# Retention's inverse root in two mixers: a power of minus one half on GpSimd instead of a root on ScalarE and a reciprocal on VectorE

## What is computed

```
def multiscale_retention(q, k, v, gate):            # 8 heads of 64, 512 tokens, chunks of 128
    ...
    o = (intra + cross).reshape(B, S, H, D)
    mu = jnp.mean(o, axis=-1, keepdims=True)
    var = jnp.mean(jnp.square(o - mu), axis=-1, keepdims=True)
    o = ((o - mu) * lax.rsqrt(var + GN_EPS)).reshape(B, S, H * D)
    return jax.nn.silu(gate) * o

def hybrid_mixer(x, ...):
    h = x @ w_in                                    # 22 tiles of 128 columns
    ...                                             # sliding-window attention, 8 heads; retention, 8 heads
    return jnp.concatenate([y_attn, y_ret], axis=-1) @ w_out
```

## Time and profile before

| | us |
|---|---|
| median of three runs | 3137.31 |
| lowest, highest | 3136.26, 3140.68 |
| the profiled execution's own time | 3135.46 |
| its span, from first to last instruction | 3134.2 |
| TensorE busy in the span | 3053.6 (97%) |
| VectorE busy | 1415.7 (45%) |
| ScalarE busy | 1173.1 (37%) |
| GpSimd busy | 373.3 (12%) |
| mean granted TensorE clock | 0.992 |

### The profile page before, as it was taken

How to read it: one execution, slowest core, us unless ns; L and a number is a source line. 1 busy time by engine, 2 the same in 40 slices (tenths; PEclk the granted TensorE clock), 3 DMA queues, 4 the chain that set the end, 5 groups by cost and what they waited for, 6 DMA issues and landing times.

```text
span 3134.2 us, 39362 instructions
## 1 busy us (share of the span) xinstructions
PE 3053.6 (97%) x16470; PEld 2554.1 (81%) x16470; DVE 1415.7 (45%) x2118; ACT 1173.1 (37%) x1910; POOL 373.3 (12%) x275
## 2 busy tenths in 40 slices
PE   8999999999999999999999999999999989999999
PEld 7888876788888888886688888899998767788888
DVE  3333465653334433356573333644423667554432
ACT  3322366442224322156553221522223456543321
POOL 0000133300001000024320000200002322110000
PEclk9999999999999999999999999999999999999999
DMA  4223321222232322331113223222233211122232
GB/s 159 95 93 92 100 88 48 75 95 94 93 93 65 121 94 91 94 112 63 61 56 120 94 89 93 68 95 95 85 88 100 81 34 34 35 94 95 94 92 76
DMA packets 76496, 269.62 MB, mean 86 GB/s; under 512 B 8720, under 2 KB 9008, under 8 KB 76064
## 3 DMA queue, kind: packets, MB, share of 16 engines
q1 hardware_dynamic: 74448, 260.08, 25.5%
q0 software_dynamic: 1872, 7.04, 0.7%
HBM read 264.97 MB, written 2.11 MB: 85 GB/s over the span
## 4 chain that ended last, share of the span: by engine, by line
PE 90%; DVE 5%; ACT 3%; issue 1%; DMA 0%; POOL 0%; SPq 0%; DVEq 0%; ACTq 0%
PE psum L376 25%; PE psum L379 25%; PE psum L382 25%; PE psum L437 3%; PE psum L449 2%; PE psum L395 1%; PE psum L399 1%; PE psum L397 1%; PE psum L673 1%; PE psum L2608 1%; DVE x_lo L740 1%; ACT prob L1766 0%; PE psum L1627 0%; PE psum L1649 0%; DVE x L825 0%
## 5 line engine op out<-in xcount | busy, mean ns | idle before, releaser
L332 DVE TENSOR_TENSOR w_lo<-w_raw,w_hi 128x1024 fp32r<-128x1024 f32 (+1 forms) x442 | 551.9, 1251 | 1246.3 <-ACT w_hi L321 1246.1
L376 PE MATMUL psum<-x_hi,w_hi 128*128 128x512 f32 (+1 forms) x2792 | 963.6, 369 | 1.9 <-ACT neg_mean L2679 1.2
L379 PE MATMUL psum<-x_hi,w_lo 128*128 128x512 f32 (+1 forms) x2792 | 947.7, 364 | 0.0
L382 PE MATMUL psum<-x_lo,w_hi 128*128 128x512 f32 (+1 forms) x2792 | 942.9, 362 | 0.0
L321 ACT CAST w_hi<-w_raw 128x1024 fp32r<-128x1024 f32 (+1 forms) x490 | 503.9, 1029 | 1160.2 <-PE psum L382 1125.4
L376 PEld LDWEIGHTS psum<-x_hi,w_hi 128*128 128x128 f32 x2792 | 499.7, 189 | 109.0 <-issue 18.3
L379 PEld LDWEIGHTS psum<-x_hi,w_lo 128*128 128x128 f32 x2792 | 498.8, 189 | 87.7 <-issue 5.5
L382 PEld LDWEIGHTS psum<-x_lo,w_hi 128*128 128x128 f32 x2792 | 499.7, 189 | 84.2
L376 PE MATMUL psum<-h_hi_ffn,w_hi 128*128 128x512 f32 (+1 forms) x792 | 296.9, 375 | 0.0
L379 PE MATMUL psum<-h_hi_ffn,w_lo 128*128 128x512 f32 (+1 forms) x792 | 292.2, 369 | 0.0
L382 PE MATMUL psum<-h_lo_ffn,w_hi 128*128 128x512 f32 (+1 forms) x792 | 290.7, 367 | 0.0
(11 more groups left out here) (384 smaller groups left out, 3428.9 us busy)
## 6 DMA issues: line engine op xcount, KB each, us to landing
w_raw<-in_ffn_gu SPq DMA_DIRECT2D x176, 512.0 KB, 3.2
w_raw<-in_ffn_down SPq DMA_DIRECT2D x64, 512.0 KB, 3.5
w_raw<-in_w_in SPq DMA_DIRECT2D x44, 512.0 KB, 3.2
w_raw<-in_b_gate SPq DMA_DIRECT2D x44, 512.0 KB, 3.2
w_raw<-in_b_up SPq DMA_DIRECT2D x44, 512.0 KB, 3.2
w_raw<-in_b_down SPq DMA_DIRECT2D x32, 512.0 KB, 3.5
w_raw<-in_ffn_down SPq DMA_DIRECT2D x32, 384.0 KB, 3.1
w_raw<-in_b_in SPq DMA_DIRECT2D x24, 512.0 KB, 3.2
```

Of the source, the lines that this page charges most:

```text
L332: nc.vector.tensor_tensor(w_lo[s][:, 0:n], w_raw[r][:, 0:n], w_hi[s][:, 0:n].bitcast(F32), ALU.subtract).then_inc(*w_low_dve.inc(u))
L376: nc.tensor.matmul(out, w_h, hi[:, c], start=first and i == 0, stop=False)
L379: nc.tensor.matmul(out, w_l, hi[:, c], start=False, stop=False)
L382: done = nc.tensor.matmul(out, w_h, lo[:, c], start=False, stop=final and i == n - 1)
```

## The change

ScalarE's step keeps its place and its input but writes the variance (Identity with the same scale and bias) where it wrote the root. VectorE's reciprocal is gone. GpSimd gets a new instruction in its place in the list, which raises the 128x512 tile to the power that stands in a constant column (-0.5, spread over the 512 columns). The constant is one more memset at the start, and GpSimd waits there for it before its next DMA. The second block and the layer norms keep their roots and reciprocals. Line numbers of the changed kernel differ by a few.

```diff
@@ timetable
-                              (e + 2.4, "r_stat", j), (e + 2.5, "o_root", j),
+                              (e + 2.4, "r_stat", j), (e + 2.5, "o_variance", j),
                               (e + 2.7, "o_inverse", j), (e + 3.2, "o_norm", j),
...
@@ mixer_act
-                    elif step == "o_root":
+                    elif step == "o_variance":
                         act.wait_ge(*o_stat.at(item))
                         nc.scalar.activation(o_sq[:], psum[:, banks["r_stat", item][0], :],
-                                             ACT.Sqrt, bias=eps[:, 1:2],
-                                             scale=1.0 / HD).then_inc(*o_root.inc(item))
+                                             ACT.Identity, bias=eps[:, 1:2],
+                                             scale=1.0 / HD).then_inc(*o_variance.inc(item))
...
@@ mixer_dve
-                    elif step == "o_inverse":
-                        dve.wait_ge(*o_root.at(item))
-                        nc.vector.reciprocal(o_sq[:], o_sq[:]).then_inc(*o_inverse.inc(item))
...
@@ mixer_pool
+                    elif step == "o_inverse":
+                        pool.wait_ge(*o_variance.at(item))
+                        nc.gpsimd.tensor_tensor(
+                            o_sq[:], o_sq[:], eps[:, 5:6].to_broadcast([P, SEQ]),
+                            ALU.pow).then_inc(*o_inverse.inc(item))
...
@@ start
+            nc.vector.memset(eps[:, 5:6], -0.5).then_inc(*eps_set.inc(8))
...
+        pool.wait_ge(*eps_set.at(8))
```

More of the change, by code:

```diff
@@ L1536, in mixer_1 @@
             o_stat = signal("o_stat", keys("r_stat"))
-            o_root = signal("o_root", keys("o_root"))
+            o_variance = signal("o_variance", keys("o_variance"))
             o_inverse = signal("o_inverse", keys("o_inverse"))
@@ L1550, in mixer_1 @@
                 "r_kv": lambda j: stated.at((j, NB - 2)), "r_out": o_made.at,
-                "r_sum": o_centred.at, "r_stat": o_root.at, "mean": leave.negated.at}
+                "r_sum": o_centred.at, "r_stat": o_variance.at, "mean": leave.negated.at}
             def pe_wait_side(step, item):
@@ L3055, in build @@
         ones_set = signal("ones_set", [0])
-        eps_set = signal("eps_set", range(8))
+        eps_set = signal("eps_set", range(9))
         start_high = signal("start_high", range(KT))
@@ L3128, in build @@
         pe.wait_ge(*half_loaded.at(0))
-        act.wait_ge(*eps_set.at(7))
-        pe.wait_ge(*eps_set.at(7))
+        pool.wait_ge(*eps_set.at(8))
+        act.wait_ge(*eps_set.at(8))
+        pe.wait_ge(*eps_set.at(8))
         act.wait_ge(*gains_loaded.at(0))
```

## The result

The changed kernel took 3737.75 us (median of four runs, 3736.76 to 3739.79) against 3138.28 us for the kernel before (four runs, 3136.26 to 3140.68): 1.191 times as long, 95% interval 1.189 to 1.192, or 599.5 us more. The prediction was 3169.7 us with a range of 3133 to 3277 us. The direction was right, the time lies far outside the range.

The account below looks back on a forecast made before the run. TensorE's own work was taken to bound the kernel. TensorE's lateness behind the power, 25.6 us in both mixers, and 6.8 us of clock made 32.4 us over 3137.31 us: 3169.7 us, range 3133 to 3277 us.

Parts of the forecast that it names:

- What bounds the kernel: TensorE's own work sets the end; edits on other engines count only through its waits, with 80.6 us idle in all.
- What is removed: VectorE loses 26.8 us of reciprocals, ScalarE 20.5 us of table loads; mostly hidden, 2.1 us won in all.
- the wait of 1.06 us: TensorE's wait at item 0 ahead of the retention's scores, for k's late `turned`; it goes without the reciprocal, in each mixer.
- The table loads: ScalarE's 16 loads of 1.283 us around the roots, 20.5 us in all, off TensorE's path except at item 0.
- What is added: GpSimd's new power, with no trace row, bounded by neighbours: 1.3 to 25.4 us, 12.7 us taken.
- P: The time of one GpSimd power over a 128x512 tile, estimated at 12.7 us, upper bound 25.4 us.
- Rival 2: The power on GpSimd takes above 25.4 us; 3276.5 us at 25.4, each further us costs eight; chance 17%.
- Where P lands: GpSimd's in-order queue makes TensorE late: 6.3 us at item 0, none at 1, 5.2 at 2, 1.3 at 3.
- The clock: TensorE's clock falls behind each new long wait, 1.7 us each, two in each mixer, 6.8 us in all.
- rival 1: The power on GpSimd is short, up to 8.5 us, and mostly hidden: 3135.2 to 3143.5 us; chance 37%.
- Rival 3: Time freed on ScalarE and VectorE reaches TensorE, so the kernel is faster, 3110.5 or 3130.6 us; chance 5%.

Follow-up runs that it names:

- e3: The changed kernel with a multiplication by the same constant column in place of GpSimd's power: 3137.06 us, ratio 1.0000 to the kernel before.
- e7: The kernel before with VectorE's reciprocal moved one place, behind k's `turned`, at items 0 to 2: 3136.27 us, ratio 0.9992.
- e2: The changed kernel with the power over the first 32 of 512 columns only: 3140.35 us, ratio 1.0008 to the kernel before.
- e1: The changed kernel with the power over the first 80 of 512 columns only: 3182.58 us, ratio 1.0142 to the kernel before.
- e4: The changed kernel with the power over 256 of 512 columns only: 3410.06 us, ratio 1.0864 to the kernel before.
- e6: The changed kernel with the power on partitions 0 to 7 only, all 512 columns: 3737.91 us in one run.
- e9: The changed kernel with the power at item 0 of each mixer only, multiplications at the other items: 3292.06 us in one run.
- e10: The changed kernel with the power at item 1 of each mixer only, multiplications at the other items: 3288.68 us in one run.

## Why the prediction was wrong

Step by step, in its own order.

- **What bounds the kernel**: right. TensorE's waits account for 577.8 of the 599.5 us, and removing work elsewhere alone (e3) changed nothing.
- **What is removed**: the wait of 1.06 us was put down to the reciprocal, and e7 shows it. That 2.1 us are then won in the whole was wrong in effect: in e3 a new wait of the same size takes its place in each mixer, and the rows point to the norm that now meets VectorE's small steps. The prediction had seen GpSimd and VectorE slow each other at item 2 and gave it no term, "since VectorE has time there"; at the maxima, which the exponentials and `v_raw` wait for, it has none (item 2 of e3, item 1 of e2). In the changed kernel the wait was gone too, and TensorE came to item 0's turn about 1 us earlier, only to wait there for the power. The table loads were off the path, as said.
- **What is added**: this step failed. The mis-sized term is P: 81.93 us, not 12.7, over three times its upper bound of 25.4. The bound was an analogy: VectorE's reciprocal against VectorE's plain pass, doubled because a power is two functions, and doubled again. It had no row of a function on GpSimd under it, and the ratio of one engine did not carry over to the other; e1, e2, e4 and e6 show a cost of 0.159 us a column whatever the partitions, so that 512 columns cost 63 plain passes. The text knew of this tail ("nothing shows that its functions are worked out in whole rows") and gave it 17%, outside the range; with no evidence against it, the range should have held it. Rival 2 had the mechanism and the rule (each us of P costs eight): from its 3276.5 us, 56.5 us more of power make 452 us more, 3729 us, against 3737.75 measured.
- **Where P lands**: right at items 2 and 3, and at item 0 in part by luck. The covers, power less wait, were forecast as 6.4, 7.5 and about 11.4 us; measured in the changed kernel 6.3, 7.6 (81.9 less 74.3) and 12.2. At item 0 the forecast counted from the turn's old start at 490.25; TensorE, freed of its 1.06 us wait, was ready about 1 us before that (at 489.94, in a trace that runs 0.66 us later here: y_lo starts at 480.56, not 479.90), which makes the wait longer, and `prob` took 1.03 us where 1.93 was assumed, which makes it shorter. In the kernel before `prob` had run beside a low part of VectorE (L332 from 487.31). At item 1 it was forecast as 13.5 and is 13.0 (82.27 less 69.3), since the wait sits at L1697; near 13 us of power that decides between a wait and none, as e1 shows.
- **The clock**: right in kind, too small. 1.7 us a wait came from a wait of 2.3 us; behind waits of some 70 us the windows give 2.6 us on average, from 1.8 to 4.4, and e9 and e10 give 2.2 and 3.9.
- **Rivals**: rival 1 (P up to 8.5) is e2, 3140.35 us, not told apart from before; the forecast for such a size was right though the power was never of it. Rival 3 falls with e3: the freed time does not reach TensorE.

## What to carry to other kernels

An operation that no trace shows on this engine has no price until it has been timed; an analogy from another engine can be wrong by a factor of six, and a single small run of it decides more than the whole working behind it. On an in-order engine the cost of a long instruction is its length less the cover of the first thing behind it that the bound engine waits for, once for each place. And a step that moves on GpSimd can land on VectorE's short steps in SBUF and give the gain back.

No version here beats the kernel before clearly. The one that points that way with a right output is e7, the reciprocal behind `turned`, at 0.9992 with an interval that includes one.

## What the runs showed of the hardware

- GpSimd's fp32 power in a tensor-tensor instruction: 0.33 us and 0.159 us a column (5.43, 13.11, 41.13 and 81.93 us for 32, 80, 256 and 512), the same for both exponents tried (-0.5 and 1.0) and both numbers of partitions (8 and 128). A product of the same shape with the same spread column took 1.04 us for 512 columns.
- During the 82 us of a power VectorE is hardly slowed. Its two-input low part in the stretch from 483 to 564 us of the changed kernel took its usual time, where beside a GpSimd product one took 2.29 us. Its steps of four columns beside item 1's power took 0.16 to 0.17 us; the one dearer row, beside the start of item 2's power, is 0.36 us (L1859 at 691.70):

```profile
L332 DVE TENSOR_TENSOR w_lo<-w_raw,w_hi 128x1024 fp32r<-128x1024 f32 x1 | 1.2, 1224 | 2.6 <-ACT w_hi L321 2.6
```

```profile
595.09 0.16 DVE L1859 TENSOR_TENSOR small<-small,gains 128x4 f32<-128x4 f32 x1
595.28 0.17 DVE L1862 TENSOR_SCALAR small<-small 128x4 f32<-128x4 f32 x1
595.49 0.16 DVE L1865 TENSOR_TENSOR small<-gains,small 128x4 f32<-128x4 f32 x1
```

- An addition of 128x4 elements on VectorE took 1.13 instead of 0.16 us when it met a GpSimd product, and ended when that did (e3); a product of 128x4 with a constant, one tensor input, took 1.19 instead of 0.17 us (e2).
- A table load on ScalarE took 1.283 us, and the next activation started 0.02 us behind it.
